# The second layer's value product turned round: V stationary in two column halves, reciprocal sums turned on TensorE

## What is computed

```python
def forgetting_attention(x, w_in, b_f, w_o):
    ...
    for n in range(S // BLOCK):
        q0, end = n * BLOCK, (n + 1) * BLOCK
        s = jnp.einsum('bqhd,bkhd->bhqk', q[:, q0:end], k[:, :end]).astype(jnp.float32) * scale
        s = s + c[:, :, q0:end, None] - c[:, :, None, :end]
        causal = jnp.arange(q0, end)[:, None] >= jnp.arange(end)[None, :]
        p = jax.nn.softmax(jnp.where(causal, s, NEG), axis=-1)
        outs.append(jnp.einsum('bhqk,bkhd->bqhd', p.astype(v.dtype), v[:, :end]))
    out = jnp.concatenate(outs, axis=1).reshape(B, S, hd_all)
    return out @ w_o
```

## Time and profile before

| What | Value |
|---|---|
| median of 3 runs | 946.93 us (946.9 to 947.31) |
| the profiled execution | 946.05 us, of which the span is 944.3 us |
| granted TensorE clock, mean | 0.986 of full speed |
| TensorE matmuls busy | 892.6 us, 95% of the span |
| VectorE busy | 540.1 us, 57% |
| ScalarE busy | 377.1 us, 40% |
| share of the chain that ended last | TensorE 88%, VectorE 5%, DMA 3% |
| value product, both layers (L652) | 68.1 us busy, 544 passes, 5.5% of the chain |
| transposes of probabilities (L635) | 43.5 us busy, 3.3% of the chain |
| transposes of the output (L660) | 10.2 us busy, 4.6 us idle before them |

### The profile page before, as it was taken

The page is one execution under the profiler, slowest core; times in us unless marked ns, Lnnn a source line. Parts: engine busy times, 40 slices in busy tenths (PEclk is TensorE's granted clock), DMA queues, the critical chain, the costliest instruction groups (busy, mean ns, idle before and its releaser), DMA issues.

```text
span 944.3 us, 12318 instructions
## 1 busy us (share of the span) xinstructions
PE 892.6 (95%) x4438; PEld 628.0 (67%) x4438; DVE 540.1 (57%) x1098; ACT 377.1 (40%) x755; POOL 125.9 (13%) x137
## 2 busy tenths in 40 slices
PE   5999999998999999989999999999999999999982
PEld 4887777884656656437878886887785566566530
DVE  3544886557776776475332224666356767667437
ACT  3322886001555555231132225777201355555300
POOL 2000332112010000041000001222111200100031
PEclk9999999998999999999999999999999999999997
DMA  9942000118999997663053222110117999999162
GB/s 314 359 171 89 2 2 1 41 48 326 355 388 377 394 390 271 213 222 137 0 185 129 90 90 108 49 47 23 67 45 281 313 373 384 394 378 368 34 212 89
DMA packets 49509, 183.14 MB, mean 194 GB/s; under 512 B 6496, under 2 KB 6496, under 8 KB 41264
## 3 DMA queue, kind: packets, MB, share of 16 engines
q1 hardware_dynamic: 35520, 132.34, 37.1%
q0 software_dynamic: 9200, 33.33, 10.8%
q10 hardware_dynamic: 4736, 16.78, 4.6%
HBM read 159.60 MB, written 22.84 MB: 193 GB/s over the span
## 4 chain that ended last, share of the span: by engine, by line
PE 88%; DVE 5%; DMA 3%; issue 2%; POOL 1%; ACT 1%; POOLq 0%; SPq 0%; DVEq 0%; ACTq 0%
PE bank L523 17%; PE bank L524 17%; PE bank L525 17%; PE bank L769 12%; PE bank L652 6%; PE bank L618 4%; PE bank L635 3%; PE bank L738 3%; PE bank L478 3%; PE bank L504 2%; PE bank L492 1%; PE bank L687 1%; DMA arena<-ys,pos 1%; PE bank L660 1%; DMA ring<-in_swa_w_in 1%
## 5 line engine op out<-in xcount | busy, mean ns | idle before, releaser
L1277 DVE TENSOR_TENSOR gu_low<-ring,gu_high 128x1024 fp32r<-128x1024 f32 x128 | 151.2, 1222 | 53.5 <-ACT gu_high L965 53.5
L965 ACT CAST gu_high<-ring 128x1024 fp32r<-128x1024 f32 x128 | 127.7, 1049 | 18.7 <-DVE arena L1412 17.6
L769 PE MATMUL bank<-ring,arena 128*96 128x512 f32 x256 | 115.8, 595 | 3.0 <-DVE arena L1402 1.8
L523 PE MATMUL bank<-gu_high,rows_high 128*96 128x512 f32 x256 | 112.3, 439 | 2.5 <-DVE rows_low L1396 2.5
L524 PE MATMUL bank<-gu_low,rows_high 128*96 128x512 f32 x256 | 101.0, 394 | 0.0
L525 PE MATMUL bank<-gu_high,rows_low 128*96 128x512 f32 x256 | 100.4, 392 | 0.0
L913 ACT ACTIVATE arena<-arena,nmax 128x256 f32<-128x256 f32 (+3 forms) x128 | 66.8, 522 | 31.0 <-DVE nmax L1208 20.2
L769 PEld LDWEIGHTS bank<-ring,arena 128*96 128x96 f32 x256 | 39.6, 165 | 55.5 <-issue 55.2
L523 PE MATMUL bank<-high,x_high 128*128 128x512 f32 x160 | 65.2, 408 | 6.9 <-DVE low L1104 5.4
L426 POOL TENSOR_TENSOR low<-ring,high 128x512 fp32r<-128x512 f32 x32 | 40.7, 1270 | 230.6 <-ACT high L933 230.6
L652 PE MATMUL bank<-arena 128*128 128x64 f32 x544 | 68.1, 269 | 0.2 <-ACT arena L927 0.2
(11 more groups left out here) (207 smaller groups left out, 1490.0 us busy)
## 6 DMA issues: line engine op xcount, KB each, us to landing
ring<-in_w_gate SPq DMA_DIRECT2D x32, 1024.0 KB, 12.5
ring<-in_w_up SPq DMA_DIRECT2D x32, 1024.0 KB, 14.7
ring<-in_w_down SPq DMA_DIRECT2D x32, 1024.0 KB, 14.9
ys<-arena ACTq DMA_DIRECT2D x32, 384.0 KB
ring<-in_fox_w_in SPq DMA_DIRECT2D x6, 2048.0 KB, 9.4
ring<-in_swa_w_in SPq DMA_DIRECT2D x3, 2048.0 KB, 10.6
ring<-in_swa_w_o SPq DMA_DIRECT2D x2, 2048.0 KB, 14.0
xd<-xres ACTq DMA_DIRECT2D x8, 512.0 KB, 2.6
```

Of the source, the lines that this page charges most:

```text
L523: eng.matmul(out, ah, wh, start=(c == 0), stop=False)
L769: mm = eng.matmul(bank[5 + half][0:CAP, :], hT[:, b, c, :], w[:, c, half * BLK:(half + 1) * BLK], start=(c == 0), stop=(c == FC - 1))
L965: eng.copy(gu_high[u % 2][:, :, part, :], slot_gate_up(use)[:, :, part, :]).then_inc(S("gu_high"), 1)
L1277: eng.tensor_tensor(gu_low[use % RING][:, :, part, :], slot_gate_up(use)[:, :, part, :], gu_high[u % 2][:, :, part, :], ALU.subtract).then ...
```

## The change

In the second layer alone, V becomes stationary: 64 columns, and the transposed probabilities stream with 128 columns (`mix_cols`). Half 0 writes partitions 0 to 63 of the bank, half 1 partitions 64 to 127, and the halves alternate block by block of the keys. The result is transposed already, so `turn_out` goes. Its sums stand in the wrong direction for the division, so VectorE writes each reciprocal 64 times side by side, 512 wide (`sums`), TensorE transposes the four blocks into free columns of banks 3 and 4 beside the next pair's first probabilities (`spread_sums`), ScalarE copies three of them and VectorE one (`take_shares`), and VectorE multiplies (`divide`). The high part is then read from SBUF and not from the bank.

```diff
--- before.py
+++ after.py
@@ -106,6 +106,7 @@
         sp = area(12288, 4 * SEQ, "p (b n) -> p b n", b=4)
         pT = area(14336, 2 * SEQ, "p (b n) -> p b n", b=2)
         heads_out = area(15360, 2 * SEQ, "p (b n) -> p b n", b=2)
+        shares = heads_out
         rtmp = area(16384, 2 * 8 * ROT, "p (a n) -> p a n", a=2)
         tok = area(6144, 2 * BLK, "p (b n) -> p b n", b=2)
         V0 = area(7168, NT * F, "p (t n) -> p t n", t=NT)
@@ -631,10 +632,39 @@
                         eng.wait_ge(S("exp_done"), 2 * STEPS * l + 2 * s + half + 1)
                         if s >= 1:
                             eng.wait_ge(S(f"pT_ready{half}"), STEPS * l + s)
+                        if l == 1 and s > NT and s % NT == 1:
+                            eng.wait_ge(S(f"shares_here{half}"), s // NT)
                         for i in range(k1 - k0):
                             mm = eng.transpose(bank[3 + half][:, i * P:(i + 1) * P],
                                                sp[:, 2 * (s % 2) + half, i * P:(i + 1) * P], ident[:, :])
+                        if l == 1 and s >= NT and s % NT == 0:
+                            if half == 0:
+                                eng.wait_ge(S("sums_ready"), s // NT)
+                            mm = spread_sums(s // NT - 1, half)
                         mm.then_inc(S("pT_done"), 1)
+
+                def spread_sums(hp, part):
+
+                    for n in ((0, 1, 2), (3,))[part]:
+                        at = P * (1 + n % 3)
+                        mm = eng.transpose(bank[3 + part][:, at:at + P], shares[:, hp % 2, n * P:(n + 1) * P], ident[:, :])
+                    return mm
+
+                def mix_cols(s):
+                    hp, n = STEP[s]
+                    k0, k1 = keys(n)
+                    if s % NT == 0 and hp >= 2:
+                        eng.wait_ge(S("o_ready"), PAIRS * l + hp - 1)
+                    for i in range(k1 - k0):
+                        for half in range(2):
+                            if i == 0:
+                                eng.wait_ge(S(f"pT_ready{half}"), STEPS * l + s + 1)
+                            v = HD * (2 * hp + half)
+                            mm = eng.matmul(bank[5 + hp % 2][HD * half:HD * half + HD, n * P:(n + 1) * P],
+                                            V[:, k0 + i, v:v + HD], pT[:, half, i * P:(i + 1) * P],
+                                            start=(i == 0), stop=(i == k1 - k0 - 1))
+                            if i == k1 - k0 - 1:
+                                mm.then_inc(S("pv_done"), 1)
 
                 def mix(s):
                     hp, n = STEP[s]
@@ -669,13 +699,20 @@
                 for s in range(STEPS):
                     turn_probs(s)
                     if s >= 1:
-                        mix(s - 1)
+                        (mix if l == 0 else mix_cols)(s - 1)
                     if s + 2 < STEPS:
                         scores(s + 2)
-                    if s >= NT and s % NT == 1:
+                    if l == 0 and s >= NT and s % NT == 1:
                         turn_out(s // NT - 1)
-                mix(STEPS - 1)
-                turn_out(PAIRS - 1)
+                if l == 0:
+                    mix(STEPS - 1)
+                    turn_out(PAIRS - 1)
+                else:
+                    mix_cols(STEPS - 1)
+                    eng.wait_ge(S("sums_ready"), PAIRS)
+                    for half in range(2):
+                        eng.wait_ge(S(f"pT_ready{half}"), STEPS * (l + 1))
+                        spread_sums(PAIRS - 1, half).then_inc(S("pT_done"), 1)
 
 
                 def route(t):
@@ -925,6 +962,14 @@
                     if s >= 1:
                         eng.wait_ge(S("pv_done"), 2 * STEPS * l + 2 * (s - 1) + 1)
                     eng.copy(pT[:, 0, 0:nk], bank[3][:, 0:nk]).then_inc(S("pT_ready0"), 1)
+                    if l == 1 and s >= NT and s % NT == 0:
+                        take_shares(s // NT - 1)
+
+                def take_shares(hp):
+
+                    if hp >= 2:
+                        eng.wait_ge(S("aT_ready"), PAIRS * l + hp - 1)
+                    eng.copy(shares[:, hp % 2, 0:3 * P], bank[3][:, P:4 * P]).then_inc(S("shares_here0"), 1)
 
                 def out_weights_high(p):
 
@@ -934,8 +979,13 @@
 
                 def out_high_part(hp):
 
-                    eng.wait_ge(S("oT_done"), PAIRS * l + hp + 1)
-                    eng.copy(attn_high[:, hp, :], bank[5 + hp % 2][:, :]).then_inc(S("aT_high"), 1)
+                    if l == 0:
+                        eng.wait_ge(S("oT_done"), hp + 1)
+                        src = bank[5 + hp % 2][:, :]
+                    else:
+                        eng.wait_ge(S("o_ready"), PAIRS * l + hp + 1)
+                        src = shares[:, hp % 2, :]
+                    eng.copy(attn_high[:, hp, :], src).then_inc(S("aT_high"), 1)
 
                 expo(0, 0)
                 expo(0, 1)
@@ -951,6 +1001,9 @@
                         out_weights_high(s // 2)
                     if s >= NT and s % NT == 2:
                         out_high_part(s // NT - 1)
+                if l == 1:
+                    eng.wait_ge(S("pT_done"), 2 * STEPS * (l + 1) + 1)
+                    take_shares(PAIRS - 1)
                 out_high_part(PAIRS - 1)
 
                 def gate_up_high(i, u, first=0, end=SPLITS):
@@ -1223,6 +1276,14 @@
                     if s >= 1:
                         eng.wait_ge(S("pv_done"), 2 * STEPS * l + 2 * (s - 1) + 2)
                     eng.tensor_copy(pT[:, 1, 0:nk], bank[4][:, 0:nk]).then_inc(S("pT_ready1"), 1)
+                    if l == 1 and s >= NT and s % NT == 0:
+                        take_shares(s // NT - 1)
+
+                def take_shares(hp):
+
+                    if hp >= 2:
+                        eng.wait_ge(S("aT_high"), PAIRS * l + hp - 1)
+                    eng.tensor_copy(shares[:, hp % 2, 3 * P:4 * P], bank[4][:, P:2 * P]).then_inc(S("shares_here1"), 1)
 
                 def normalise(hp):
 
@@ -1241,10 +1302,25 @@
                                       bank[5 + hp % 2][:, :].rearrange("p (n h d) -> p n h d", n=NT, h=2),
                                       ri.unsqueeze(3).to_broadcast([P, NT, 2, HD]), ALU.mult).then_inc(S("o_ready"), 1)
 
+                def sums(hp):
+
+                    eng.wait_ge(S("exp_done"), 2 * STEPS * l + 2 * NT * (hp + 1))
+                    if hp >= 2:
+                        eng.wait_ge(S("aT_ready"), PAIRS * l + hp - 1)
+                    eng.reciprocal(shares[:, hp % 2, :].rearrange("p (n h d) -> p n h d", n=NT, h=2),
+                                   rsum[:, hp % 2, :, :].unsqueeze(3).to_broadcast([P, NT, 2, HD])).then_inc(S("sums_ready"), 1)
+
+                def divide(hp):
+
+                    eng.wait_ge(S("pv_done"), 2 * STEPS * l + 2 * NT * (hp + 1))
+                    for part in range(2):
+                        eng.wait_ge(S(f"shares_here{part}"), hp + 1)
+                    eng.tensor_tensor(shares[:, hp % 2, :], bank[5 + hp % 2][:, :], shares[:, hp % 2, :], ALU.mult).then_inc(S("o_ready"), 1)
+
                 def evac_out(hp):
 
                     eng.wait_ge(S("aT_high"), PAIRS * l + hp + 1)
-                    eng.tensor_tensor(attn_low[:, hp, :], bank[5 + hp % 2][:, :],
+                    eng.tensor_tensor(attn_low[:, hp, :], bank[5 + hp % 2][:, :] if l == 0 else shares[:, hp % 2, :],
                                       attn_high[:, hp, :], ALU.subtract).then_inc(S("aT_ready"), 1)
 
                 if l == 0:
@@ -1256,16 +1332,23 @@
                     evac_heads(GROUPS[0] - 1)
                 for s in range(STEPS):
                     evac_probs(s)
+                    if l == 1 and s % NT == NT - 1:
+                        sums(s // NT)
                     if s + 2 < STEPS:
                         for half in range(2):
                             mask_and_max(s + 2, half)
                     if l == 0 and s % NT == 1:
                         shift_sinks(s // NT)
                     if s >= NT and s % NT == 0:
-                        normalise(s // NT - 1)
+                        (normalise if l == 0 else divide)(s // NT - 1)
                     if s >= NT and s % NT == 2:
                         evac_out(s // NT - 1)
-                normalise(PAIRS - 1)
+                if l == 0:
+                    normalise(PAIRS - 1)
+                else:
+                    eng.wait_ge(S("pT_done"), 2 * STEPS * (l + 1) + 2)
+                    take_shares(PAIRS - 1)
+                    divide(PAIRS - 1)
                 evac_out(PAIRS - 1)
 
 
```

## The result

The changed kernel takes **975.88 us** (975.57 to 976.43), the one before 947.12 in the same comparison: ratio 1.0302, 95% interval 1.0289 to 1.0314, 28.8 us slower. The sign was forecast; the size was 19, at 966, with 952 to 979 as the range.

A forecast was written before the change was run, and what follows sets the result against it. TensorE, busy for 10.75 of a pair's 10.75 us, was taken to set the pace. The profiled 946.05 + 14.4 for waits + 5 for the clock gave 965.5; with the median 0.9 above that execution, 966 us, range 952 to 979.

The forecast's parts named there:

- The value product: TensorE, second layer's attention: both column halves run at once, so a pair's value products take 2.94 us instead of 4.61.
- The reciprocal: VectorE: widening from 8 to 512 columns makes it 3.35 us, at 6.25 ns a column.
- Where it stands: The reciprocal's place in VectorE's queue: TensorE waits for it inside the next pair's first transposes, idle for 2.9 us.
- the walk: One attention pair followed wait by wait across the engines: period from 10.73 to 12.65 us, +1.92, seven times, +13.4.
- The end: After the last pair, up to the output projection: the eighth reciprocal's wait costs +1.0 us.
- The clock: TensorE's clock halves behind the new gaps: +5 us, half of the bounds 0 and 10 (8 x 1.2).
- cheap-reciprocal rival: VectorE's 512-column reciprocal costs only a plain operation's 0.69 us: 939.7 us in all; chance 0.09.
- a longer reciprocal: Rival: VectorE's 512-column reciprocal takes 4.3 us, adding 7.6, 974 us in all; chance 0.10.
- halves in turn: Rival: TensorE's column halves take turns, so the value product gains nothing: 978 us with the clock; chance 0.16.

The follow-up runs named there:

- e3: e1 with the value product doing all key blocks of half 0, then all of half 1, instead of alternating: 943.71 us.
- e4: e1 with the first 256 of the 512 columns from a wide reciprocal, the others from the small one and a copy: 956.73 us.
- e7: The change with the transposes of the reciprocals moved two steps later and the 512-column reciprocal behind the next masks: 977.97 us.
- e2: The change with 16 unused bf16 multiplications (14 at the end) filling TensorE's wait for the reciprocals: 964.21 us.
- e1: The change with a reciprocal of the pair's 8 sums, copied 64 times side by side, instead of one of 512 columns: 943.25 us.
- e5: e1 with the reciprocals transposed two steps later, two blocks in each bank, and the small reciprocal and VectorE's copy behind the next masks: 943.99 us.
- e8: e1 with ScalarE, in the second layer, taking the next step's second exponential before copying the transposed probabilities: 943.23 us.
- e9: e8 with two reciprocal blocks in each bank, so ScalarE copies 256 columns instead of 384: 943.52 us.
- e11: e9 with the value product doing all key blocks of half 0, then all of half 1: 943.77 us.
- e12: e1 with two reciprocal blocks in each bank and ScalarE's second exponential ahead of the copy in only one of every four steps: 939.49 us.
- e6: e5 with GpSimd instead of VectorE copying the small reciprocal 64 times side by side: 945.08 us.

## Why the prediction was right, and where it was short

- *The value product.* Right: 1.02 us for 16 passes, 1.05 forecast from the scores' row halves, and 2.78 a pair against 2.94: 0.21 to 0.22 for each block of keys and 0.16 a step, not 0.21. The column halves do work at once (e3). The row behind the price of a pass has 96 stationary columns and not the full 128, which the sum did not say; 1.82 / 16 gives the same 0.11. The Trainium skill's rule, that weight loads overlap matmuls only where the row group differs (TensorE: Matmul & The Clock Gate, What overlaps and what doesn't), does not describe these column halves: the loads of the 16 passes are busy for 0.85 of the 1.02 us (609.73, L663), so they run beside the passes.
- *The reciprocal.* Right: 3.342 us against 3.35. A slope from 4 to 8 columns carried to 512, where it could have failed. By the Trainium skill's repeat count of 8 (VectorE: DVE Perf Modes, First, the fixed hardware budget) 4.3 was estimated; the trace shows 6 periods of its 0.96 GHz a column, as the row before did.
- *Where it stands.* Right: the gap is in T0, 2.62 us of idle time (2.9 forecast), and time ahead of it is passed on whole (e4). The reason was half told: the walk spoke of TensorE's wait first. e7 shows that with this wait moved away VectorE's queue makes as long a gap one step later.
- *The walk.* 12.65 forecast, 13.05 in e2, where the clock is full: 0.4 a pair too short, 2.8 in all. Its order of waits and its hand-overs were right, within 0.1 us up to the spread. What it had too short are the transposes behind a wait. In each of the four groups the time from the last release to the product behind is 0.15 longer than its price of 0.11 a transpose: in T3 half 1 is released at 616.74 and M0 starts at 617.33, 0.59 and not 0.44. That is 0.6 a pair, less the 0.16 by which the products were shorter than forecast. The end was right: +1.0 forecast; from M1 to the projection 5.08 us instead of 3.98, so 1.1 (the items of the prediction's 4.1 add up to 4.0).
- *The clock.* This is the term that was mis-sized. I took +5 as half of bounds of 0 and 10. It cost **11.7** (e2), above my upper bound. Every gap made the clock fall, not half of them. A fall cost the 1.2 forecast in five pairs and 2.3 in the two where it lasted twice as long, 1.5 on average. And the 1.6 us that the projection's start costs behind the last gap were not in the bound at all. The prediction also says that the trace has one such gap. The trace before has more, and they point both ways:

```profile
216.52 2.69 PE L687 MATMUL bank<-wr,xT 128*128 128x16 f32 x16 [0.87 <-DVE xT L1071]
218.00:219.00 1.00, 1.00 (x6) 1.00 (x7) 0.00 (x0) 0.00 (x0) 0.00 (x0) 0.50 0.97 381
...
912.68 0.67 PE L504 MATMUL bank<-arena 128*128 128x512 f32 x1 [1.86 <-DMA arena<-ys,pos]
914.00:916.00 2.00, 2.00 (x6) 0.76 (x4) 1.29 (x2) 0.00 (x0) 1.45 (x2) 1.00 0.87 313
```

  Behind two gaps of 0.73 and 0.87 us with matmuls of 16 columns around them the clock fell; behind one of 1.86 us it did not. The length of a gap alone does not decide.
- *The cheap-reciprocal rival* gave 939.7 with a period of 9.9; e1, the nearest to it that was built (its reciprocal and copy take 0.66 us together), has 10.36 and took 943.25. So its sign was right, from the same walk with the same shortfall: 7 x 0.46 = 3.2 of the 3.6.

14.4 + 2.8 for the walk is 17.2, and e2, where the clock does not fall, is 17.1 us slower than before. The 11.7 for the clock are the rest by their making. That the time lies in the stated range is in part luck: the forecast's own range was 955 to 971, and 952 to 979 only took in two rivals, a longer reciprocal and halves in turn, of which neither came true.

What stays open: whether e1, e3, e5, e8, e9 and e11 differ at all in the whole. Their medians are 943.2 to 944.0 where their periods, 10.29 to 10.58, would make up to 2 us. That is hardly more than can be told: the intervals are 1.1 to 1.8 us either way, and e1's own executions range from 939.84 to 945.70. One source of such differences lies outside the stage. Between 214 and 226 us the mean granted clock is 0.72 in e8's profiled execution and 0.86 in e9's, and e8 reaches its first M3 of the second layer at 581.29, e9 at 580.13. Where the clock falls, and for how long, differs there although the code up to that point is the same. What decides it is open, and so is why e12 gains more in the whole than its period says. And a chain of scores, masks, exponentials and transposes that closes on itself would explain why so much of the shorter product comes back; e8 shows one wait that moved, the rest is argued from the timelines, not shown.

## What to carry to other kernels

Do not broadcast into an expensive elementwise operation: take the reciprocal of the few numbers and copy the result. One instruction decided here between 3% slower and 0.4% faster. When a change puts idle time on a TensorE that was dense, price the clock for every gap, and for the stage behind the last one, and read in the trace how long each fall lasts. And when the busiest engine gets shorter, look at what its length had been covering: of the 1.83 us that the product saves in a pair 0.37 reached the period in e1, and 0.63 in e12, after two other engines' work had been fitted to it.

## What was not expected of the hardware

- Two fp32 products with 64 stationary columns each, on the two column halves, run at once when they alternate in the queue: 1.02 us for 16 passes of 128 columns. All of one half and then all of the other takes 1.51 (e3), still less than the 1.76 of 16 passes at 0.11; why is open.
- A reciprocal on VectorE takes 6.25 ns a column: 8 columns 0.19 to 0.20 (0.145 right behind another reciprocal, e4), 256 columns 1.742, 512 columns 3.342 us. The copy of 8 numbers 64 times side by side takes 0.427 on VectorE and 0.62 on GpSimd (e6, median).
- Seven idle stretches of 2.62 us and one of 2.39 brought TensorE from 2.4 to 1.2 GHz each time, and so did one of 1.87 at the end of e6. Of seven stretches of 1.61 us in e4 one did, and its pair was 1.16 us longer; one of 1.86 in the kernel before did not, and there the clock also fell behind stretches of 0.73 and 0.87.
